# Where the modulation products stand in TensorE's order during attention: ahead of the turning of the weights or behind the outputs

## What is computed

```python
s = einsum('bqhcd,bkhcd->bchqk', q, k) * (ATT_HEAD_DIM ** -0.5)
p = softmax(s, axis=-1)
a = p[:, 0] - lam * p[:, 1]
return einsum('bhqk,bkhe->bqhe', a, v)
```

```python
mod_l = split(c_act @ ada_w[l] + ada_b[l], 6)
mod_c = split(cc_act @ ada_w[l] + ada_b[l], 6)
```

## Time and profile before

| | |
|---|---|
| median of 3 runs | 2467.14 us (2466.2 to 2467.89) |
| profiled execution | 2466.14 us |
| its span, first to last instruction | 2464.4 us |
| mean granted TensorE clock | 0.992 |
| TensorE busy (matmul) | 2393.4 us, 97% |
| TensorE busy (weight load) | 2044.9 us, 83% |
| VectorE / ScalarE / GpSimd busy | 1093.4 / 1068.3 / 1603.4 us |
| chain that ended last: share of TensorE | 87% |

### The profile page before, as it was taken

The page is one execution under the profiler, slowest core; times in us unless marked ns, Lnnn a source line. Parts: engine busy times, 40 slices in busy tenths (PEclk is TensorE's granted clock), DMA queues, the critical chain, the costliest instruction groups (busy, mean ns, idle before and its releaser), DMA issues.

```text
span 2464.4 us, 37279 instructions
## 1 busy us (share of the span) xinstructions
PE 2393.4 (97%) x14828; PEld 2044.9 (83%) x14828; DVE 1093.4 (44%) x2091; ACT 1068.3 (43%) x1987; POOL 1603.4 (65%) x1364
## 2 busy tenths in 40 slices
PE   8999999999999999999999999999998999989998
PEld 7779998896588888887888888888958888889997
DVE  3545513053755667657342112131375676673211
ACT  2346534114644767674032002043264666654643
POOL 1018875872075778778875888865406788887886
PEclk9999999999999999999999999999999999999999
DMA  7557544325734444435323323333364444375564
GB/s 219 179 176 193 167 118 126 103 81 195 267 95 131 120 129 119 128 103 180 103 69 103 100 89 103 99 96 98 119 227 122 120 129 136 111 186 158 172 203 137
DMA packets 379311, 339.42 MB, mean 138 GB/s; under 512 B 14448, under 2 KB 343698, under 8 KB 378130
## 3 DMA queue, kind: packets, MB, share of 16 engines
q1 hardware_dynamic: 361586, 298.80, 40.4%
q10 hardware_dynamic: 16992, 38.02, 5.5%
q0 software_dynamic: 576, 0.43, 0.2%
HBM read 329.62 MB, written 7.61 MB: 137 GB/s over the span
## 4 chain that ended last, share of the span: by engine, by line
PE 87%; POOL 4%; DVE 3%; ACT 2%; issue 2%; DMA 2%; SPq 0%; ACTq 0%; POOLq 0%; DVEq 0%
PE PS L751 41%; PE PS L1167 13%; PE PS L1176 5%; PE PS L809 5%; PE PS L1367 3%; POOL rounded L2824 3%; PE PS L774 3%; PE PS L1224 2%; PE PS L702 2%; PE PS L1081 1%; PE PS L1208 1%; PE PS L1285 1%; PE PS L973 1%; PE PS L1069 1%; DMA ring<-in_w_down_dram 1%
## 5 line engine op out<-in xcount | busy, mean ns | idle before, releaser
L2824 POOL TENSOR_TENSOR rounded<-ring,rounded 128x512 fp32r<-128x512 f32 (+1 forms) x872 | 1115.8, 1313 | 485.0 <-ACT rounded L1419 371.6
L751 PE MATMUL PS<-rounded 128*128 128x256 f32 (+1 forms) x6096 | 1048.1, 334 | 15.7 <-DVE mid_a L2529 5.0
L751 PEld LDWEIGHTS PS<-rounded 128*128 128x128 f32 x6096 | 929.9, 191 | 129.8 <-issue 13.6
L2847 POOL TENSOR_TENSOR rounded<-ring,constants 128x512 fp32r<-128x512 f32 x216 | 230.9, 1099 | 236.4 <-PE PS L751 113.4
L1167 PE MATMUL PS<-rounded 128*128 128x512 f32 (+1 forms) x1536 | 346.8, 382 | 2.3 <-DVE mid_a L2580 1.8
L1167 PEld LDWEIGHTS PS<-rounded 128*128 128x128 f32 x1536 | 274.4, 189 | 58.1 <-issue 6.4
L1419 ACT ACTIVATE rounded<-ring 128x2048 fp32r<-128x2048 f32 (+1 forms) x99 | 180.1, 1823 | 123.9 <-DMA ring<-in_w_mlp_dram 44.4
L2566 DVE SCALAR_TENSOR_TENSOR mid_a<-PS,V,mid_a 128x510 f32<-128x510 f32 (+3 forms) x256 | 182.6, 713 | 71.5 <-ACT mid_a L1764 64.6
L1176 PE MATMUL PS<-rounded 128*128 128x512 f32 (+1 forms) x768 | 140.8, 340 | 0.0
L2029 ACT ACTIVATE PS<-PS 128x512 f32<-128x512 f32 (+1 forms) x64 | 30.4, 475 | 251.7 <-DVE PS L2737 251.6
L1176 PEld LDWEIGHTS PS<-rounded 128*128 128x128 f32 x768 | 117.9, 189 | 18.1 <-issue 3.6
(11 more groups left out here) (283 smaller groups left out, 3046.9 us busy)
## 6 DMA issues: line engine op xcount, KB each, us to landing
ring<-in_w_mlp_dram SPq DMA_DIRECT2D x64, 1024.0 KB, 5.3
ring<-in_w_in_dram SPq DMA_DIRECT2D x56, 1024.0 KB, 5.5
ring<-in_ada_w_dram SPq DMA_DIRECT2D x48, 1024.0 KB, 5.3
ring<-in_w_in_dram SPq DMA_DIRECT2D x81, 512.0 KB, 4.1
ring<-in_w_up_dram SPq DMA_DIRECT2D x44, 512.0 KB, 5.2
big<-decay_sums ACTq DMA_DIRECT2D x40, 512.0 KB, 5.4
ring<-in_w_ssd_o_dram SPq DMA_DIRECT2D x16, 1024.0 KB, 5.9
ring<-in_w_out_dram SPq DMA_DIRECT2D x12, 1024.0 KB, 5.0
```

The source lines that it names most:

```text
L751: mm = pe.matmul(PS[:, b, 0:cols], w[:, k, m * P:(m + 1) * P], x(half * kt + k), start=(half == 0 and k == 0 and n_pass == 0), stop=(half ...
L2824: ins = pool.tensor_tensor(lo[:, r], raw[:, r], hi[:, r], ALU.subtract)
L2847: ins = pool.tensor_tensor(hi[:, r], raw[:, r], ones[:, 0:1].broadcast_to([P, 512]), ALU.mult)
```

## The change

The modulation product of iteration u is issued after the scores of unit u+2 and ahead of the turning of unit u, in place of after the outputs of unit u-1. It is the same in the first block and in both layers of the second. No other engine's program changes.

```diff
@@ first block
             for u in range(n_u + 1):
                 if u + 2 < n_u:
                     scores1(u + 2)
+                if u in mods_of[0]:
+                    mod_rows_of(mods_of[0][u])
                 if u < n_u:
                     turn_weights(u, 4, prob[:, u % 2, 0:T] if UNITS1[u][0] == "A" else None)
                 if u >= 1:
                     outputs1(u - 1)
-                if u in mods_of[0]:
-                    mod_rows_of(mods_of[0][u])
@@ second block, each layer
                 for u in range(n_u + 1):
                     if u + 2 < n_u:
                         scores2(u + 2)
+                    if u in mods:
+                        mod_rows_of(mods[u])
                     if u < n_u:
                         turn_weights(u, TT if units[u][1] < LT else LT)
                     if u >= 1:
                         outputs2(u - 1)
-                    if u in mods:
-                        mod_rows_of(mods[u])
```

## The result

The changed kernel takes 2473.15 us (median of 16 runs, 2460.49 to 2481.96), the kernel before 2467.04 us (16 runs): ratio 1.0029, 95% interval 1.0018 to 1.0041. It is slower, by 6 us where 3.5 were forecast. Measured once more beside a fresh set of the kernel before it gave 2472.42 against 2467.28, ratio 1.0020 (1.0010 to 1.0031). By means over the runs the two sets are 6.9 and 5.1 us apart from theirs. The time of 2473.15 lies inside the range that was given, but "no change that can be told" was the likeliest case, and what can be told is a loss.

A forecast was written before the change was run, and what follows sets the result against it. TensorE was taken to set the pace, with 8.6 us of waits before turnings. First block 0.3, layer 0 2.4 and layer 1 0.8 summed to +3.5 us on the 2467.14 median: 2470.6 us, range 2466.5 to 2474.0.

The forecast's parts named there:

- no change that can be told: Whole kernel: time within 0.2% of the kernel before; chance 0.78.
- T(u) starts no sooner than 1.63 us after O(u-2), 1.36 for a short unit: Layer 0: turning unit u's weights waits on a VectorE chain, 1.63 us (long) or 1.36 (short) after unit u-2's outputs.
- The terms: Attention stretches: added turning waits of +0.3 us in the first block, +2.4 in layer 0, +0.8 in layer 1.
- the copies of finished products: Layer 0, units 11 and 27: VectorE copying products just ahead of their chain adds 0.25 us each, +0.5 together.
- The neighbours at 0: TensorE, all 48 moved products: new neighbouring groups of another shape cost 0, with bounds of 0.10 us per product either way.
- The rival of dearer shape changes: Scores to product and product to turning cost 0.10 us more per product, 4.8 on top: 2475.4 us; chance 0.13.
- ScalarE's slack: Layer 0: 0.5 us to spare before scores wait for exponentials, costing nothing; if used up, +1.4 us, 2472.0; chance 0.06.
- The slots: Products' waits for loaded weights, now ahead of turning and outputs, cost nothing, with over 4 us to spare.
- The rival of a swallowed delay: After the stretches, later loads or roundings already set the pace, so the added waits vanish: 2467.1 us; chance 0.10.
- the last waits: Final turning of each stretch loses its covering product and waits 1.1 to 1.6 us, +1.0 us per stretch.
- the bound of 4.9 us: Whole kernel: a measurement tells about 0.2%, 4.9 us, from no change.
- 0.16 for slower: Whole kernel measurably slower: 0.13 for dearer shape changes plus 0.03 for a forecast landing above the 0.2% bound.

The follow-up runs named there:

- layer 0 alone: Kernel before, with products moved between scores and turning in layer 0 only, the old order elsewhere: ratio 1.0023 (1.0015 to 1.0032).
- the last product behind: Changed kernel, but the last modulation product of each of the three stretches is again issued after the outputs: 2469.69 us, ratio 1.0020.
- halves: Changed kernel with each product cut into two slices of rows, spread so every unit has something between scores and turning: 2462.96 us, ratio 0.9995.
- layer 0 alone with filler: Kernel before with the new order in layer 0 only, plus two unused matmuls inside that layer's last turning's wait: ratio 0.9999.
- the changed kernel with filler: Changed kernel plus two matmuls with unused results in the wait of the last unit of each stretch: 2467.03 us, ratio 1.0008.
- the first block alone: Kernel before with the new product order in the first block only, the old order in both layers: ratio 1.0003 (0.9994 to 1.0013).
- last product ahead: Kernel before with only the last product of each of the three stretches moved ahead of the turning: 2469.51 us, ratio 1.0016.
- the variants of layer 0: Kernel before with layer 0 alone altered: new order plus filler matmuls, 0.9999; only its last product ahead, 0.9999; new order with its last product after outputs, 1.0007.

## Why the prediction was right and where it was wrong

*The rule "T(u) starts no sooner than 1.63 us after O(u-2), 1.36 for a short unit": right.* The waits of the profile after follow from it place by place: units 3, 7, ... in layer 0 with 0.66, the last turnings with 1.17, 1.36 and 1.63. One small wait that it left standing, 0.17 us at unit 14 of the first block, did not come.

*The terms: right in sum.* Named waits rose by 0.2, 2.1 and 1.0 us, +3.3 in all, where the terms gave +0.3, +2.4 and +0.8. At equal clock the kernel is 3.7 to 3.9 us slower, with a standard error of 0.6 to 0.8, +3.5 forecast; layer 0 alone 2.0, forecast 2.4. One term was nothing: the copies of finished products, +0.5 us. The seven waits of 0.66, the 0.56 at unit 30 and the 1.36 at unit 31 already make up the 6.5 us of layer 0, so units 11 and 27 wait no longer than the others.

*The neighbours at 0: right.* Product to turning is 1.00, scores to product 0.63 and 1.05. The rival of dearer shape changes is out.

*ScalarE's slack: right.* TensorE's wait for ScalarE before scores in layer 0 is 0.9 us once, at the start, as before.

*The slots: right.* TensorE named no wait for a load before a product.

*The rival of a swallowed delay: out.* At equal clock the whole of it arrives at the end.

*The step that failed* is the one from the time to "no change", and it has two parts.

One was never written down as a term: that TensorE's clock stays as it was. The prediction read "at full clock" from the windows of the kernel before, called the last waits 1.1 to 1.6 us long, and priced each at its own length. The runs show a mean clock 0.0007 under the control's in the set of the changed kernel that has one, worth 1.3 us with a standard error of 1.0; 0.0017 under it with only the last product of each stretch moved, worth 3.2 us; and 0.0026 under it with layer 0 alone changed, worth 5. The second of these shows that uncovered last turnings can lower the clock; in layer 0 the same move alone did not (0.9924 for 0.9924). How much of the whole change's +5.1 and +6.9 us it makes is open, between about 1 and 3 us.

The other is the bound of 4.9 us under which nothing was to be told. The intervals reached only some 0.11% to either side, 2.8 us, so a loss of the forecast size, 0.14%, could already stand clear of 1. It did for the kernel with the last product behind: 1.0020 (1.0009 to 1.0032) with a clock 0.0004 under its control's and no fall behind either attention in its profile. The chance of 0.78 for "no change" rested on a margin of 1.4 us between forecast and bound, with nothing for the clock in it and a bound that was too wide. 0.16 for slower was too little; the size of the waits was right.

## What to carry to other kernels

Work that is meant to fill a wait belongs between the operations whose gap it covers, but what counts is how evenly it is cut: whole products moved from one side to the other only moved the gaps, halves closed those inside the loop. Follow such a move to the last unit of the loop: the shift by one place opens a hole there that no steady-state argument shows. And where a change makes TensorE idle for a microsecond more at the end of a stretch, leave room in the range for the granted clock, and compare kernels by means over many runs with the clock beside them.

## What the hardware showed that was not expected

- The granted clock fell to half although no single idle time in the 40 us before it was longer than 1.4 us in layer 0 and 1.2 us in the first block; in the profile of layer 0 alone with filler it fell after idle times of at most 0.66 us, and where one of 1.8 us stands behind the first block, in the changed kernel with filler, it did not. The Trainium skill, TensorE: Matmul & The Clock Gate, Why this matters for your kernels, warns of idle gaps between bursts of matmuls. The trace agrees in so far as gaps stood before both long falls of the changed kernel, but they were short, two to four of them within 8 us (in the changed kernel 1.17 and 0.47 in the first block; 0.56, 1.36, 0.54 and 0.44 in layer 0). What sets it off is open.
- Behind the first block's attention it fell for 10.2 us in all four profiles whose last turning was bare (changed kernel twice, the first block alone, last product ahead), and in one of the other ten, for 3.4 us. Over the twelve runs of the first block alone it cost hardly anything all the same (0.0009 of clock, ratio 1.0003). Why the profiled executions are so uniform and the timed ones are not is open.
- Behind layer 0's attention it fell in some executions of the same order and not in others: for 13.7 us in the first profile of the changed kernel and not in the second, and for 13.7 or 17 us in three of the variants of layer 0.
- Every one of the fourteen profiles has falls elsewhere too, most of 3.4 or 6.8 us. All falls together are 38.7 us at half clock in the kernel before and 61.8 and 42.9 in the two profiles of the changed one (one less the mean clock, times the span, times two).
- The scatter of the changed kernel (5.2 and 3.0 us) goes for the most part with the clock: time and mean clock have a correlation of -0.89 in its first 16 runs and -0.93 in the nine later ones.
